# Triangular inversion in the delta-rule mixer: block transposes on VectorE in place of a third matrix product up to blocks of 32

## What is computed

```
kkt = einsum("bhnid,bhnjd->bhnij", kb, k) * decay
A   = eye(C) + where(strict, kkt, 0)          # unit lower triangular
sol = triangular_solve(A, [v*beta, kb*exp(gc)], lower=True, unit_diagonal=True)
u, w = sol[..., :DV], sol[..., DV:]
v_new = u - w @ S;  o = q_dec @ S + qk @ v_new;  S = S*g_last + k_tail^T @ v_new
```

## Time and profile before

| | |
|---|---|
| time, median of 3 runs | 1613.39 us (1612.88 to 1613.64) |
| profiled execution, span from first to last instruction | 1610.6 us |
| what lies around the span (median less span) | 2.8 us |
| mixer, 367 to 780 us of the span | 413 us |
| TensorE busy | 1533.3 us, 95% of the span |
| VectorE busy | 716.2 us, 44% |
| mean granted TensorE clock | 0.980 of full speed |

### The profile page before, as it was taken

One profiled execution on the slowest core, in us unless ns is written; L12 is line 12 of the kernel. 1 busy time (PEld: TensorE's weight loads), 2 busy tenths in 40 slices (PEclk: granted clock), 3 DMA queues, 4 the chain that ended last, 5 costly groups with the idle time before them and its releaser, 6 DMA issues.

```text
span 1610.6 us, 23009 instructions
## 1 busy us (share of the span) xinstructions
PE 1533.3 (95%) x9003; PEld 1398.8 (87%) x9003; DVE 716.2 (44%) x1132; ACT 351.4 (22%) x569; POOL 132.0 (8%) x200
## 2 busy tenths in 40 slices
PE   5999999998999999998899999999999999999997
PEld 3799899997888888886598999989898989989896
DVE  5356544534566666565333333342424333332415
ACT  5354533231111111111120211112020211111012
POOL 1000000001222222211000000000000000000001
PEclk7999999997999999999899999999999999999999
DMA  5012122162122211122170201111010102010002
GB/s 195 14 43 85 53 105 91 66 209 79 40 66 65 65 59 40 64 72 72 63 277 27 75 25 57 32 46 52 26 52 26 52 26 78 26 52 26 0 0 111
DMA packets 52561, 105.12 MB, mean 65 GB/s; under 512 B 4784, under 2 KB 30320, under 8 KB 52528
## 3 DMA queue, kind: packets, MB, share of 16 engines
q1 hardware_dynamic: 52528, 104.67, 18.8%
HBM read 82.66 MB, written 22.00 MB: 65 GB/s over the span
## 4 chain that ended last, share of the span: by engine, by line
PE 45%; issue 2%; ACT 1%; DVE 1%; DMA 1%; POOL 0%; DVEq 0%; ACTq 0%; POOLq 0%
PE bank L86 15%; PE bank L88 15%; PE bank L87 15%; ACT gu_hi L1592 1%; DMA out_y<-y_out 1%; DVE acc L1678 0%; DVE y_out L1642 0%; DVE hf L1654 0%; ACT y_out L1628 0%; POOL fstat L1693 0%; DVEq L1677 0%; ACTq L75 0%; POOL fstat L1691 0%; POOLq L1510 0%; DVE gu_lo L1635 0%
## 5 line engine op out<-in xcount | busy, mean ns | idle before, releaser
L86 PE MATMUL bank<-ht_hi,w_hi 128*128 128x364 f32 (+1 forms) x576 | 190.4, 330 | 0.0
L88 PE MATMUL bank<-ht_hi,w_lo 128*128 128x364 f32 (+1 forms) x576 | 189.4, 329 | 0.0
L87 PE MATMUL bank<-ht_lo,w_hi 128*128 128x364 f32 (+1 forms) x576 | 189.4, 329 | 0.0
L1654 DVE TENSOR_TENSOR hf<-sg,bank 128x364 f32<-128x364 f32 (+1 forms) x66 | 35.1, 532 | 342.9 <-PE bank L88 340.8
L86 PE MATMUL bank<-ht_hi,gu_first_hi 128*128 128x364 f32 (+1 forms) x528 | 173.4, 328 | 1.4 <-PEq L842 1.4
L87 PE MATMUL bank<-ht_lo,gu_first_hi 128*128 128x364 f32 (+1 forms) x528 | 173.3, 328 | 0.0
L88 PE MATMUL bank<-ht_hi,gu_lo 128*128 128x364 f32 (+1 forms) x528 | 173.2, 328 | 0.0
L86 PE MATMUL bank<-ht_hi,gu_hi 128*128 128x364 f32 (+1 forms) x528 | 173.1, 328 | 0.0
L87 PE MATMUL bank<-ht_lo,gu_hi 128*128 128x364 f32 (+1 forms) x528 | 173.1, 328 | 0.0
L88 PE MATMUL bank<-ht_hi,gu_first_lo 128*128 128x364 f32 (+1 forms) x528 | 173.0, 328 | 0.0
L1678 DVE TENSOR_TENSOR acc<-acc,bank 128x512 f32<-128x512 f32 (+1 forms) x198 | 132.3, 685 | 90.3 <-PE bank L88 90.3
(11 more groups left out here) (267 smaller groups left out, 2458.6 us busy)
## 6 DMA issues: line engine op xcount, KB each, us to landing
w_raw<-in_w_in SPq DMA_DIRECT2D x24, 512.0 KB, 4.2
dn_raw<-in_w_down SPq DMA_DIRECT2D x22, 512.0 KB, 4.3
scratch_qkv<-cb_y SPq DMA_DIRECT2D x12, 512.0 KB, 2.7
qkv_in<-scratch_qkv SPq DMA_DIRECT2D x8, 768.0 KB, 6.3
gu_first_raw<-in_w_gate SPq DMA_DIRECT2D x11, 512.0 KB, 3.5
gu_first_raw<-in_w_up SPq DMA_DIRECT2D x11, 512.0 KB, 4.3
gu_raw<-in_w_gate SPq DMA_DIRECT2D x11, 512.0 KB, 3.5
gu_raw<-in_w_up SPq DMA_DIRECT2D x11, 512.0 KB, 4.3
```

What stands on the lines that cost most here:

```text
L86: pe.matmul(out, w_hi, x_hi, start=start, stop=False)
L87: pe.matmul(out, w_hi, x_lo, start=False, stop=False)
L88: return pe.matmul(out, w_lo, x_hi, start=False, stop=stop)
L1654: eng.tensor_tensor(hf[b][:, 0:m], sg[b][:, 0:m], psum[2 * b + 1][:, 0:m], ALU.mult).then_inc(hf_done, 1)
```

## The change

`BLOCK` = 32 is new. VectorE has a transpose that turns each 32 x 32 block of a tile in place, without moving blocks (STREAM_TRANSPOSE in the lists below). As long as the inverse consists of blocks of at most 32 on the diagonal, this is its transpose.

- u is transposed by VectorE into `y_` (used as a scratch), in two halves, and `pp` is masked from there; L1001 and the semaphore of its bank go.
- y comes from x by two VectorE transposes; the TensorE transposes of `pp` (L1010) go.
- At levels with LEVELS[q] = 2, 4, 8 and 16 (q = 1 to 4) the product X isn't formed. After y -= Y, VectorE waits for its own result and transposes y into x. At q = 5 (32) nothing changes, and q = 6 never had an X. For the samples, X goes at q = 1.

```diff
+BLOCK = 32
@@ TensorE, chunk
-                eng.wait_ge(m_["u_done"], c + 1)
-                for h in range(H):
-                    mm = eng.transpose(psum[4][0:n, h * P:h * P + n], u_[0:n, h, 0:n], ident[0:n, 0:n])
-                mm.then_inc(m_["ut_tr"], 1)
                 if tail:
                     project(tail, rg_steps[5:])
                 eng.wait_ge(m_["mix_done"], c)
                 eng.wait_ge(m_["mq_done"], c + 1)
-                for r in range(2):
-                    eng.wait_ge(m_["pp_done"], 2 * NL * c + r + 1)
-                    for h in (2 * r, 2 * r + 1):
-                        mm = eng.transpose(psum[Y_BANK[r]][0:n, h * P:h * P + n], pp[0:n, h, 0:n], ident[0:n, 0:n])
-                    mm.then_inc(m_["y_tr"], 1)
...
-                        if not last:
+                        if LEVELS[q] >= BLOCK and not last:
                             for h in (2 * r, 2 * r + 1):
                                 mm = eng.matmul(psum[X_BANK[r]][0:n, h * P:h * P + n], y_[0:n, h, 0:n],
                                                 pp[0:n, h, 0:n], start=True, stop=True)
@@ VectorE, chunk
-                eng.wait_ge(m_["ut_tr"], c + 1)
                 eye = over(ident[0:n, 0:n], n)
+                eng.wait_ge(m_["u_done"], c + 1)
                 for r in range(2):
-                    eng.tensor_tensor(pair_of(pp, n, r, n), pair_of(b4(4), n, r, n), mlow2(0, n),
+                    eng.transpose(pair_of(y_, n, r, n), pair_of(u_, n, r, n)).then_inc(m_["ut_done"], 1)
+                for r in range(2):
+                    eng.wait_ge(m_["ut_done"], 2 * c + r + 1)
+                    eng.tensor_tensor(pair_of(pp, n, r, n), pair_of(y_, n, r, n), mlow2(0, n),
                                       ALU.mult).then_inc(m_["pp_done"], 1)
...
                 for r in range(2):
-                    eng.wait_ge(m_["y_tr"], 2 * c + r + 1)
-                    eng.tensor_tensor(pair_of(y_, n, r, n), eye[:, 0:2], pair_of(b4(Y_BANK[r]), n, r, n),
-                                      ALU.subtract).then_inc(m_["y_done"], 1)
+                    eng.wait_ge(m_["x_done"], 2 * (NL - 1) * c + r + 1)
+                    eng.transpose(pair_of(y_, n, r, n), pair_of(x_, n, r, n)).then_inc(m_["y_done"], 1)
...
-                        if not last:
-                            eng.wait_ge(m_["x_mm"], 2 * (NL - 2) * c + 2 * (q - 1) + r + 1)
+                        if LEVELS[q] >= BLOCK and not last:
+                            eng.wait_ge(m_["x_mm"], 2 * c + r + 1)
                         eng.tensor_tensor(pair_of(y_, n, r, n), pair_of(y_, n, r, n), pair_of(b4(Y_BANK[r]), n, r, n),
                                           ALU.subtract).then_inc(m_["y_done"], 1)
-                        if not last:
+                        if last:
+                            continue
+                        if LEVELS[q] < BLOCK:
+                            eng.wait_ge(m_["y_done"], 2 * NL * c + 2 * q + r + 1)
+                            eng.transpose(pair_of(x_, n, r, n), pair_of(y_, n, r, n)).then_inc(m_["x_done"], 1)
+                        else:
                             eng.tensor_tensor(pair_of(x_, n, r, n), pair_of(x_, n, r, n),
                                               pair_of(b4(X_BANK[r]), n, r, n), ALU.subtract).then_inc(m_["x_done"], 1)
```

More of the change, by code:

```diff
@@ L773, in mixer_block @@
              "kt_tr kt_done gr_done d_mm e_done e2_done ml_done kg_done ktail_done kk_mm qk_mm u1_done mq_done u_done "
-             "ut_tr pp_done y_tr y_done x_done p_mm y_mm x_mm w_mm nw_done v_mm o1_mm vnew_done o2_mm ds_mm s_done "
+             "ut_done pp_done y_done x_done p_mm y_mm x_mm w_mm nw_done v_mm o1_mm vnew_done o2_mm ds_mm s_done "
              "t1_done o_done osq_done so_done fac_done on_done on_tr mix_done mixhi_done mixlo_done "
```

## The result

The changed kernel takes 1602.36 us (median of 4 runs, 1601.84 to 1602.98) against 1613.14 (1610.96 to 1613.64) for the kernel before on the same chip: a ratio of 0.9939 [0.9925, 0.9953]. The medians differ by 10.8 us where 12.6 had been predicted; the ratio makes it 9.8. The time lies in the range (1597 to 1605) that the prediction gave its likeliest case. The profiled execution has a span of 1600.4 us against 1610.6, 10.2 us less, and what follows takes those 10.2 us apart.

A forecast was written before the change was run, and what follows sets the result against it. TensorE's list was taken to bound mixer chunks, with VectorE's chain limiting the gain. Seven chunks at 1.40 (9.8), chunk 0 (1.7) and samples (1.1) sum to 12.6 us: 1613.4 to 1600.8, own range 1597 to 1605.

The forecast's parts named there:

- the start: Start of the inversion, chunk with a tail: nothing won, first Y later by 0.37 us, of which 4d = 0.16.
- three steps: Y to Y in the levels with both slots: 3.69 us against 4.07, three such steps giving 1.14 us a chunk.
- the step to level 5: The step without slot 0, chunk with a tail: 2.98 us against 3.61, a gain of 0.63.
- d: What a VectorE transpose of 256 columns takes beyond 0.34 us; taken as +0.04, about 100 d in all.
- chunk 0: Chunk without slots: level 2.98 us after 3.44, four times 0.46 less 4d at the start, 1.7 us won.
- The samples: Samples' inversion: X of one level and the mix_lo wait go; with part of the transposes 1.1 us won.
- the wait for mix_lo that was to go: In the samples: TensorE's 0.46 us wait goes, since VectorE no longer waits for TensorE's transposes there.
- What follows the mixer starts earlier by the same amount: Behind the mixer: work bound by TensorE simply starts earlier by the 12.6 us won.
- Rival 1: Clock falls around the first P, 3 us lost each time; 1622 if in all seven chunks, 1611 in half; chance 0.20.
- Rival 2: VectorE's transpose is slow as the scan: d = 0.24, 20 us worse than forecast, 1621; chance 0.10.
- Rival 3: VectorE's chain in the levels costs 0.08 us more per half level, giving back 7 us, 1608; chance 0.10.
- Rival 4: In the levels, a wait on one's own result costs nothing: P of pair 1 0.22 earlier, 7 us more, 1594; chance 0.06.

The follow-up runs named there:

- experiment 3: Changed kernel with a second, useless VectorE transpose (of y into pp) ahead of each transpose in the levels; 1619.9 us, ratio 1.004.
- 6: Changed kernel with slot 0 (levels 2 to 4) between the two P and slot 1 (levels 1 to 3) between the two Y; 1600.34 us, ratio 0.992.
- experiment 9: Changed kernel with mq behind the first masks, slots between the pairs, and level 3's addition to x_in between its two masks; 1587.44 us, ratio 0.9842.
- Experiment 1: Only the start changed against the kernel before (VectorE transposes of u and x), X kept at every level; 1616.28 us, ratio 1.0015.
- experiment 11: Changed kernel with six useless matmuls ahead of TensorE's wait for mix, before the first P of prompt chunks; 1597.59 us, ratio 0.9905.
- experiment 4: Changed kernel whose level transposes read long-ready pp in place of y, without the wait on VectorE's own result (wrong inverse, same work); 1592.23 us, ratio 0.9872.
- experiment 2: Only the levels changed against the kernel before; the start keeps TensorE's transposes; 1597.81 us, ratio 0.9905.
- 5: Changed kernel with six useless matmuls behind TensorE's wait for mix, ahead of the first P; 1597.63 us, ratio 0.9917.
- 7: Changed kernel with mq (mask of the query products) moved from ahead of u's transposes to behind the first P's masks; 1595.21 us, ratio 0.9895.
- 8: Only the levels changed against the kernel before, with the slots moved between the pairs; 1594.57 us, ratio 0.9887.
- 10: Only the levels changed, slots between the pairs, level 3's addition to x_in moved between the two masks; 1591.01 us, ratio 0.9864.

## Why the prediction was right, and where it was not

**The mechanism was right:** X goes, the chain through VectorE becomes the bound of levels 1 to 4, and half of what the removal of X could give is won there (0.43 of 0.88 a level). Y to Y was forecast at 3.69 (3.6 to 3.8) and is 3.64; the idle ahead of P at 1.5 and is 1.39; experiment 3 shows the chain bare, and 6 and 9 that TensorE could do a level in 3.3.

**Terms that were mis-sized.** Per chunk with a tail 1.40 was forecast, 1.90 came: the start lost 0.10 in place of 0.37, three steps gave 1.28 for 1.14, the step to level 5 0.68 for 0.63, 0.04 the rest. At the start 0.16 of the 0.27 is d, counted four times at 0.04 and measured 0.00; the rest lies in the prices, since the two masks take 0.63 for 0.68 and mix_lo to its product 0.70 for 0.74. In the levels it is not d, which is 0.03 there: y of the second pair to its transpose takes 0.41 for 0.45. One price has no row: the 0.48 from the second P, which had waited, to the slot behind it (the earlier trace rows give 0.44 and 0.55). From the second transpose to that slot 0.46 + 0.48 = 0.94 was taken, and it is 513.39 - 512.42 = 0.97. Experiment 1 gives the start's loss on its own (0.12).

In chunk 0 1.7 was forecast and 0.72 came. TensorE's busy time there fell by 3.1 us, but the clock's mean is 0.79 against 0.84. TensorE is at 1.2 GHz when the chunk begins, and the new idle falls into that stretch and is longer there:

```profile
383.56 2.04 PE L1011 MATMUL bank<-inv,u 128*128 128x128 f32 x8 [2.53 <-DVE inv L1285]
```

Before, it was 0.61 us ahead of the transposes of pp. In windows of 1 us the clock goes up between 389 and 390 us, in the kernel before between 385 and 386: some 3.4 us more at 1.2 GHz. With the filler of experiment 11 it goes up between 382 and 383, and the chunk takes 38.94.

The samples gave 1.27 for 1.1, but in part not for the reason given: the wait for mix_lo that was to go is still there (0.46 before),

```profile
719.88 0.50 PE L87 MATMUL bank<-wo_hi,mix_hi 128*128 128x512 f32 x1 [0.45 <-DVE mix_lo L1231]
```

so that step of the prediction failed. What came instead: with TensorE's transposes of u and pp gone, this first slot starts 719.88 - 709.94 = 9.94 us behind the sums and no longer 731.47 - 720.72 = 10.75, which is 0.81; the other 0.46 is the X of one level (0.44 forecast).

**"What follows the mixer starts earlier by the same amount" failed too.** From the start of the samples to the end the changed kernel is 0.58 us longer, though the samples' own stretch is 1.27 shorter: 1.85 lost behind it. One stretch of 3.4 us at half clock is new there, with TensorE busy throughout, which makes up to 1.7 of it (half of 3.4). Busy time by stretch:

```profile
792.00:794.00 2.00, 2.00 (x10) 2.00 (x9) 0.53 (x1) 1.31 (x3) 0.00 (x0) 0.63 0.65 203
```

It begins behind a wait that both kernels have, 1.43 us here and 1.44 before,

```profile
791.64 0.41 PE L87 MATMUL bank<-ht_hi,gu_first_hi 128*128 128x364 f32 x1 [1.43 <-PEq L843]
```

and which before was followed by no fall. The same idle may or may not bring one.

**The total is closer than its terms.** Undisturbed chunks gave 13.25 for 9.8 and the samples 0.17 more than forecast; the two falls took 2.24, chunk 0 gave 0.98 less, 1.85 were lost behind the samples and 0.95 ahead of the mixer: 12.6 + 3.45 + 0.17 - 2.24 - 0.98 - 1.85 - 0.95 = 10.2. That the sum comes within 2.4 us of the span's difference is in good part luck.

**Rival 1 (the clock falls behind the new idle, 0.20) came true in part,** in two chunks of seven. The first, around the idle and behind it:

```profile
590.00:592.00 2.00, 1.04 (x5) 0.53 (x3) 2.00 (x7) 0.00 (x0) 0.36 (x1) 1.00 0.00 0
592.00:593.00 1.00, 0.57 (x5) 0.57 (x6) 1.00 (x4) 0.63 (x1) 0.00 (x0) 1.00 0.00 0
...
594.00:595.00 1.00, 0.98 (x3) 0.82 (x4) 0.63 (x2) 0.00 (x0) 0.00 (x0) 0.77 1.14 342
595.00:596.00 1.00, 1.00 (x6) 0.94 (x5) 0.00 (x0) 0.00 (x0) 0.00 (x0) 0.50 0.70 162
```

The clock falls some 2 us after the first P has ended the idle (1.5 to 2.1 us in experiments 1, 3, 4 and 6), with the shorter wait of 0.43 us for mix_lo in between. Its price was mis-sized: 3 us had been taken from a stretch of 6.83 us at half clock; these last 3.4, and part of what they slow had been waiting for VectorE, so they cost 1.14 and 1.10 (0.8 to 1.6 in the experiments). In all seven chunks it would be 8 us, less than the 12.6 of the forecast: at its true price this rival could not have reached the slower side. Over all profiles, with the idle at 1.4 us (the changed kernel, experiments 1, 3, 4, 6) there are 8 falls in 35 chunks; with it filled or at most 1.1 us (2, 5, 7 to 11) none in 49, and none in the seven of the kernel before (0.57). Experiment 11 differs from the changed kernel in that idle alone and keeps the wait of 0.43; but 2 falls of seven against none, by one profile of each, could be chance. It is the count over all kernels that ties the falls to the idle. What picks the chunks in which they happen stays open.

**Rival 2** (the transpose as slow as the scan) is refuted by the 413 ns. **Rival 3** (0.08 us more each half level) too: Y to Y is below the forecast, not above. (Its 7 us were counted high: two half levels in each of four levels and eight chunks are 64, which makes 5 us.) **Rival 4** (the wait on one's own result costs nothing) is refuted by the 0.46 against 0.34 and by experiment 4, whose 0.88 us a chunk is what the rival's arithmetic had set on that wait (4 times 0.22).

## What to carry to other kernels

Work taken off a busy engine is won only down to the chain through the other one: find where that chain is late, and put there the independent work that stood elsewhere (experiment 9 does so without removing an instruction; of the 13.1 us between its span and that of the changed kernel 8.3 are shorter chunks, 2.2 the falls that are gone and 1.4 chunk 0), moving every operation that isn't urgent to a place where its engine waits anyway. Of a change in several parts, time each: here one half (experiment 2) beats the whole, since the other half frees only time that TensorE then idles away, and where there is such an idle the clock is low for longer. A term that moves the clock is priced by how long the low level lasts and by how much of that stretch was TensorE's path.

## What the runs showed of the hardware

- VectorE's block transpose of 128x256 fp32 takes 413 ns, like an elementwise operation of that size (0.41), and 434 to 445 just behind the subtraction in the levels.
- An operation on 256 columns that waits for the result of the one just before it starts 0.11 to 0.12 us later than one that doesn't (experiment 4: 0.34 for 0.46, 0.30 for 0.41).
- Idles of 1.4 us on TensorE in dense work were followed by 3.4 us at 1.2 GHz in 8 of 35 chunks, idles of at most 1.1 us in none of 49. With useless products in the idle there were no such falls, and chunk 0, in which the clock is low at first, took 38.94 us in place of 40.61.
